# Loading only the weight columns that are used, in a chunked scan of two head groups

## The reference

```
h = rms_norm(x);  proj = h @ w_in
HGRN2 heads (4):   scores[t,s] = sum_d q[t,d] k[s,d] exp(b[t,d] - b[s,d]), s <= t
                   o = scores @ v + (q exp(b)) @ state
DeltaNet heads (4): (I + lower(beta k k^T decay)) solved for u and w, chunk by chunk
                   v_new = u - w @ state;  o = q @ state + attn @ v_new
x += rms_norm(concat(o_a, o_b) @ w_out)
x += rms_norm(gated MLP with a causal convolution (1024 -> 2 x 2816 -> 1024))
x += rms_norm((p @ w_ple) * sigmoid(x @ w_ple_gate))
```

## Time and profile before

| | us |
|---|---|
| three runs | 1464.81, 1464.89, 1466.47 (median 1464.89) |
| the profiled execution, its own time | 1465.47 |
| its span, first to last instruction | 1463.7 |
| scan, from the end of the front to the first matmul of the output projection | about 432 to 596 |
| mean granted TensorE clock, share of full | 0.987 |

### The profile page before, as it was taken

One profiled execution on the slowest core, in us unless ns is written; L12 is line 12 of the kernel. 1 busy time (PEld: TensorE's weight loads), 2 busy tenths in 40 slices (PEclk: granted clock), 3 DMA queues, 4 the chain that ended last, 5 costly groups with the idle time before them and its releaser, 6 DMA issues.

```text
span 1463.7 us, 19613 instructions
## 1 busy us (share of the span) xinstructions
PE 1424.8 (97%) x7167; PEld 1202.3 (82%) x7167; DVE 1029.9 (70%) x1512; ACT 704.1 (48%) x1297; POOL 227.8 (16%) x242
## 2 busy tenths in 40 slices
PE   5999999999999999999999999999999999999996
PEld 4877888878879999888888888888888888888885
DVE  6666545553118888447997999999999685677566
ACT  5432457412226887436774344444445444454434
POOL 3000001100017767110000000000000154310010
PEclk8999999999997999999999999999999999999998
DMA  8553424544712333454442335335326755424222
GB/s 215 86 106 44 43 61 127 152 108 101 165 59 86 100 104 95 143 188 148 148 122 87 103 100 171 116 115 173 107 81 237 249 196 189 137 80 133 84 100 101
DMA packets 156318, 181.52 MB, mean 124 GB/s; under 512 B 21240, under 2 KB 96190, under 8 KB 156222
## 3 DMA queue, kind: packets, MB, share of 16 engines
q1 hardware_dynamic: 155968, 180.16, 42.5%
q10 hardware_dynamic: 254, 0.10, 0.0%
HBM read 130.95 MB, written 49.28 MB: 123 GB/s over the span
## 4 chain that ended last, share of the span: by engine, by line
PE 93%; DVE 3%; ACT 1%; DMA 1%; issue 1%; POOL 0%; SPq 0%; ACTq 0%; DVEq 0%; POOLq 0%
PE psum L2263 10%; PE psum L2264 10%; PE psum L2265 10%; PE psum L563 5%; PE psum L564 5%; PE psum L565 5%; PE psum L1202 5%; PE psum L2202 4%; PE psum L2204 4%; PE psum L2203 4%; PE psum L2175 4%; PE psum L2176 4%; PE psum L2177 4%; PE psum L1256 3%; PE psum L618 3%; PE psum L619 3%
## 5 line engine op out<-in xcount | busy, mean ns | idle before, releaser
L148 DVE TENSOR_TENSOR w_wlo<-w_raw,w_whi 128x1024 fp32r<-128x1024 f32 x70 | 93.8, 1340 | 254.6 <-ACT w_whi L142 254.5
L2263 PE MATMUL psum<-m_hi,w_whi 128*128 128x512 f32 x416 | 162.4, 390 | 1.5 <-issue 0.7
L142 ACT ACTIVATE w_whi<-w_raw 128x1024 fp32r<-128x1024 f32 x70 | 74.0, 1057 | 184.8 <-PE psum L2177 85.4
L2265 PE MATMUL psum<-m_hi,w_wlo 128*128 128x512 f32 x416 | 161.9, 389 | 0.0
L2264 PE MATMUL psum<-m_lo,w_whi 128*128 128x512 f32 x416 | 161.8, 389 | 0.0
L563 PE MATMUL psum<-h_hi,w_whi 128*128 128x512 f32 x320 | 127.0, 397 | 3.7 <-DVE h_lo L834 3.7
L565 PE MATMUL psum<-h_hi,w_wlo 128*128 128x512 f32 x320 | 125.4, 392 | 0.0
L564 PE MATMUL psum<-h_lo,w_whi 128*128 128x512 f32 x320 | 125.4, 392 | 0.0
L2202 PE MATMUL psum<-w_whi,g_slot 128*128 128x512 f32 x308 | 120.1, 390 | 0.6 <-DVE w_wlo L2979 0.6
L2204 PE MATMUL psum<-w_whi,g_slot 128*128 128x512 f32 x308 | 119.8, 389 | 0.0
L2203 PE MATMUL psum<-w_wlo,g_slot 128*128 128x512 f32 x308 | 119.8, 389 | 0.0
(11 more groups left out here) (374 smaller groups left out, 3485.6 us busy)
## 6 DMA issues: line engine op xcount, KB each, us to landing
w_raw<-in_w_up SPq DMA_DIRECT2D x39, 512.0 KB, 3.9
w_raw<-in_w_in SPq DMA_DIRECT2D x36, 512.0 KB, 6.5
s_rows<-pair_work SPq DMA_DIRECT2D x11, 1024.0 KB, 4.1
w_raw<-s_rows SPq DMA_DIRECT2D x44, 256.0 KB, 2.7
g_rows<-pair_work SPq DMA_DIRECT2D x18, 512.0 KB, 2.7
w_raw<-g_rows SPq DMA_DIRECT2D x33, 256.0 KB, 3.2
w_raw<-in_w_out SPq DMA_DIRECT2D x16, 512.0 KB, 4.2
mixed_home<-in_w_down SPq DMA_DIRECT2D x32, 256.0 KB, 3.9
```

What stands on the lines that cost most here:

```text
L2263: pe.matmul(out, wh[:, part], hi(kt), start=(start and kt == 0), stop=False)
L2265: ins = pe.matmul(out, wl[:, part], hi(kt), start=False, stop=(stop and kt == KT // 2 - 1))
```

## The change

Ten products per chunk get weights with fewer columns, and rows of the result with no use are neither computed nor copied. For score level n the weights are the first 128 - 2^(n-1) key columns: 127, 126, 124, 120, 112, 96, 64. Of the inverse, dt32 loads the first 96 columns, dt64 the first 64, y64 the last 64 (its result stands in partitions 64 to 127 of the bank). y32 and dx keep their 128. The copies by DVE and ACT out of these banks are cut to the same partitions. Moving operands, counts of instructions, order, semaphores and transfers stay as they were.

```diff
--- before.py
+++ after.py
@@ -1087,6 +1087,7 @@
     SCORE_BANK = (0, 7, 3, 6, 1, 7, 2, 7)
     BANK_OF = {"ks": 2, "solve": 3, "gd": 3, "og": 4, "oh": 5, "hd": 3, "turn": 2, "mix_g": 2, "mix_h": 5,
                "y32": 6, "dx": 6, "dt32": 1, "y64": 6, "dt64": 7}
+    DT_ROWS, Y64_ROWS = (slice(0, P - SB), slice(0, 2 * SB)), slice(2 * SB, P)
     FIRST_BANK_OF = {"y32": 4, "dx": 5, "dt32": 6, "y64": 4, "dt64": 6}
 
     def __init__(self, nc, k, a, front, shared, heads_on):
@@ -1125,6 +1126,10 @@
     def packed(self, ap):
 
         return ap[:, 0:NH * P // 2].rearrange("p (h t) -> p h t", h=NH)
+
+    def live_keys(self, n):
+
+        return slice(0, P - (1 << (n - 1)))
 
     def packed_blocks(self, ap, m):
 
@@ -1194,12 +1199,12 @@
     def bank(self, name, c):
         return (self.BANK_OF if c else self.FIRST_BANK_OF)[name]
 
-    def pe_products(self, pe, key, bank, left, right, live=None):
-
-        out = self.banks.open(pe, key, bank)
+    def pe_products(self, pe, key, bank, left, right, live=None, rows=slice(0, P)):
+
+        out = self.banks.open(pe, key, bank)[rows, :]
         columns = lambda ap: ap if live is None else self.half(ap, *live)
         for h in range(NH):
-            ins = pe.matmul(columns(self.hs(out, h)), left(h), columns(right(h)), start=True, stop=True)
+            ins = pe.matmul(columns(self.hs(out, h)), left(h)[:, rows], columns(right(h)), start=True, stop=True)
         self.multiplied.mark(ins, key)
 
     def pe_y32(self, pe, c):
@@ -1213,7 +1218,7 @@
         self.banks.released(pe, ("y32", c))
         pe.wait_ge(self.s["xt_in"], (c + 1) * 16)
         self.pe_products(pe, ("dt32", c), self.bank("dt32", c), lambda h: self.hs(self.y, h), lambda h: self.hs(xt, h),
-                         (SB, 1))
+                         (SB, 1), self.DT_ROWS[0])
 
     def pe_dx(self, pe, c):
         xt = self.xt[c % 2]
@@ -1223,13 +1228,13 @@
         self.banks.released(pe, ("dx", c))
         self.banks.released(pe, ("dt32", c))
         self.pe_products(pe, ("y64", c), self.bank("y64", c), lambda h: self.hs(self.lt, h), lambda h: self.hs(self.x, h),
-                         (2 * SB, 0))
+                         (2 * SB, 0), self.Y64_ROWS)
 
     def pe_dt64(self, pe, c):
         xt = self.xt[c % 2]
         self.banks.released(pe, ("y64", c))
         self.pe_products(pe, ("dt64", c), self.bank("dt64", c), lambda h: self.hs(self.y, h), lambda h: self.hs(xt, h),
-                         (2 * SB, 1))
+                         (2 * SB, 1), self.DT_ROWS[1])
 
     def pe_first_inverse(self, pe, step):
 
@@ -1252,8 +1257,9 @@
             pe.wait_ge(s["levels"], c * LEVELS + n)
             at = (c * LEVELS + n - 1) % 3
             out = self.banks.open(pe, ("score", c, n), self.SCORE_BANK[n])
+            live = self.live_keys(n)
             for h in range(NH):
-                ins = pe.matmul(self.packed(out)[:, h, :], hs(self.kl[at], h), self.packed(self.ql[at])[:, h, :],
+                ins = pe.matmul(self.packed(out)[live, h, :], hs(self.kl[at], h)[:, live], self.packed(self.ql[at])[:, h, :],
                                 start=True, stop=True)
             self.multiplied.mark(ins, ("score", c, n))
         else:
@@ -1369,7 +1375,8 @@
             return
         m, key = (SB, 2 * SB)[level], (("y32", "y64")[level], c)
         self.done(act, key)
-        half = lambda ap: self.blocks(heads(ap), m, 0)
+        rows = self.Y64_ROWS if level else slice(0, P)
+        half = lambda ap: self.blocks(heads(ap), m, 0)[rows]
         self.banks.release(act.activation(half(self.y[:]), half(self.banks.of(key)), ACT.Copy), key)
 
     def act_exp(self, act, c, lv):
@@ -1502,8 +1509,10 @@
             self.banks.released(dve, ("dt32", c))
         else:
             self.done(dve, ("dx", c))
-        self.banks.release(dve.copy_predicated(self.blocks(heads(xt[:]), m, 1), self.mask_for(self.k.mask[:, LEVELS - 2 + level, :], m, 1),
-                                               self.blocks(heads(self.banks.of(key)), m, 1)), key)
+        rows = self.DT_ROWS[level]
+        self.banks.release(dve.copy_predicated(self.blocks(heads(xt[:]), m, 1)[rows],
+                                               self.mask_for(self.k.mask[:, LEVELS - 2 + level, :], m, 1)[rows],
+                                               self.blocks(heads(self.banks.of(key)), m, 1)[rows]), key)
 
     def dve_dx(self, dve, c):
         if c >= NT:
@@ -1534,8 +1543,9 @@
         if n:
             self.banks.released(dve, ("score", c, n - 1))
             m = 1 << (n - 1)
-            ins = dve.copy_predicated(self.blocks(heads(self.sc[:]), m, 1), self.mask_for(k.mask[:, n - 1, :], m, 1),
-                                      self.packed_blocks(self.banks.of(key), m))
+            live = self.live_keys(n)
+            ins = dve.copy_predicated(self.blocks(heads(self.sc[:]), m, 1)[live], self.mask_for(k.mask[:, n - 1, :], m, 1)[live],
+                                      self.packed_blocks(self.banks.of(key), m)[live])
         else:
             ins = dve.copy_predicated(heads(self.sc[:]), over_heads(k.ident[:].bitcast(U32)), heads(self.banks.of(key)))
         self.banks.release(ins, key)
```

## The result

The changed kernel takes **1458.49 us** in the median of 4 runs (1456.2 to 1459.18); beside it the kernel before took 1465.68 in 4 (1464.81 to 1467.18). The ratio is 0.995, with a 95% interval of 0.9937 to 0.9962. So it is faster by 7.2 us where 14.3 were forecast, and 1458.49 lies 2 us above the range. The profiled execution took 1458.11 us (span 1456.4), 7.36 less than that of the kernel before.

A forecast was written before the change was run, and what follows sets the result against it. PE bounds the kernel, paced by weight loads at 0.112 us a record. Savings of 0.99 (first inverse), 1.92 (chunk 0), 10.80 (chunks 1 to 6) and 0.60 us (chunk 7) total 14.3: 1450.6 us, range 1447.8 to 1456.5.

The forecast's parts named there:

- What a shorter load is worth: Scan, per chunk: shorter loads of the scores and inverse save 1.80 us, period 19.92 to 18.12 us.
- chunks 1 to 6: Middle of the scan: six chunks at 1.80 us each, 10.80 us saved.
- the price of a column: PE weight loads: each column left out saves 0.83 ns a record, with 0.87 as upper bound.
- Rival 2: Changes between wide and narrow weights cost 0.16 us a pair, 24 pairs, 3.9 us back: 1454.5 us; chance 0.12.
- rival 3: PE empties at each width change, 96 columns included: 40 groups, 0.66 us a pair, 1476.9 us; chance 0.03.
- Rival 1: DVE becomes the bound at 18.9 us a chunk; total gain 9.5 us, 1455.4 us; chance 0.11.
- Rival 4: The 112 ns pace is not the load's, so nothing changes: 1464.9 us; chance 0.05.
- The floor of 63 ns a record: 64-column groups: a record falls from 112 to 63 ns, not 59, saving 0.39 us a group.
- First inverse: Between the projection's slabs, where PE is full: 0.21 + 0.39 + 0.39 = 0.99 us saved.
- Chunk 0: Start of scan: levels 5 to 7, partly at half clock, plus next chunk's dt32 and y64, save 1.92 us.
- the 2 us allowed for it: Start of scan: PE's half-speed clock stretch could end sooner or later, 2 us either way.
- Chunk 7: Earlier savings vanish in PE's wait for DVE before the mixer's turn; levels 6 and 7 behind it save 0.60 us.

The follow-up runs named there:

- four pairs against one: Changed kernel with level 7's four 64-column heads alternating with the mixer's four 128-column transposes in chunks 1 to 7: 1464.54 us, ratio 0.9989.
- the best version: Changed kernel with level 7 and dt64 loading 65 columns, y64 still its last 64: 1453.57 us, ratio 0.9914, period 18.48 us.
- the kernel with 65 columns: Changed kernel with level 7 and dt64 loading 65 columns and y64 all 128: 1454.9 us, ratio 0.9924.

## Why the prediction was wrong

**The step that failed** is in the sum, "What a shorter load is worth": level 7, y64 and dt64 were priced by their eight loads alone, 0.39 us each, with nothing for the two ends of the group. Each end pair costs 0.29 us (0.29 from four pairs against one, 0.285 from 64 against 65 columns, 0.28 from the best version). In chunks 1 to 6, 18 of them are 5.2 of the 5.48 us that are missing (10.80 - 5.32); most of the rest is the price of a column (below). For the whole kernel 24 x 0.29 = 7.0, and 14.3 - 7.0 = 7.3 beside the 7.36 between the two profiled executions, but that this fits so closely is luck: two of the 24 pairs are hidden by chunk 7's wait, and smaller errors make up for them.

**Rival 2 was the mechanism, priced at about half.** It had the 24 pairs and where they lie. Its price, 0.16, was taken from the small transposes, and against a cost at a change of width I held, under rival 3, where 8-column matmuls sit among wide ones without a gap. Those rows are fp32r, the changed groups are plain fp32, and the experiments show that for fp32r even 64 columns are free. I did weigh their 512 moving columns as a reason for doubt; the number type, though I had named it beside the earlier trace rows, I did not weigh, and it was the one that mattered.

**Rival 3**, a drain at every change of width including 96 columns, and slower than before: wrong in both. 96 columns pay nothing (0.70 us a group), and a pair costs 0.29 and not 0.66, under the 0.36 from which it would have decided.

**Rival 1**, DVE: it had room. PE waits for it nowhere in chunks 1 to 6, neither in the changed kernel nor in the version with a period of 18.48. **Rival 4**, a pace that is not the load's: refuted by 0.80 and 0.70 us for 112 and 96 columns.

**Point by point.** The price of a column: load durations give 0.86 ns, near the 0.83 taken, but the pace gained less. Levels 1 to 6 and dt32 brought 0.56 of 0.63 us in their own experiment, and the kernel with 65 columns 1.30 of 1.47: 0.74 ns a column in both. The reason is the first load of each shortened group, which still takes the 0.11 us of the wide one ahead (the first two loads of 65 columns above end after 0.25 us, each of them lasting 0.14), so that seven records of eight gain; 7/8 of 0.83 is 0.73. The floor of 63 ns a record: too high, a group of 65 columns takes 0.53 us, 0.11 to its second record and then 7 x 0.06; by itself that would have made the gain larger.

The Trainium skill ("TensorE: Matmul & The Clock Gate", LDWEIGHTS), whose columns divided by 1.2 GHz the prediction weighed, gives an estimate of 54 ns for 65 columns; the 60 seen agree to 6.

First inverse: 0.99 forecast; PE left its last slab 0.38 us earlier (431.59 to 431.21), which is 0.99 less two pairs to 0.03, and 0.10 of that went into a longer wait for ACT's hgrn_q (0.94 to 1.04 us).

Chunk 0: 1.11 against 1.92, and its terms can't be told apart. Its forecast held 0.39 for y64 of chunk 1. That group lies behind the mark, in the next period, which leaves 1.53; and since chunks 1 to 6 were given a y64 each as well, this one was in truth chunk 7's, which stands ahead of chunk 7's wait and saves nothing. One pair, level 7's, makes it 1.24. The clock then moved: level 7 ran at half speed before (455.66 to 457.36) and at full speed after (455.60 to 456.21; granted 1.00 from 455 to 456, where it was 0.50), while from 447 to 449 the clock was lower after (granted 0.50 for 0.96). In all, half-speed time by the windows was 12.6 + 4.4 us and is 15.5 + 1.6 (granted 0.63 and 0.96), the same 17 us, so the 2 us allowed for it were not needed.

Chunk 7: the longer wait before the turn came as forecast, 0.60 for 0.28, but that its 0.59 us in all agree with 0.60 is luck. From the mark to the end of that wait it took 9.24 us and not 9.41 (572.91 to 582.15, 579.63 to 589.04): 0.17 gained where nothing was forecast. Behind it 0.42 was gained: 0.18 by level 6, 0.09 by level 7 with its ends (what level 7 and the turn behind it save in the middle of the scan), and some 0.14 by a shorter idle stretch ahead of the last HGRN2 outputs.

DVE's waits for PE were to be nearly gone, and they are not: from 473 to 593 us 3.7 us are left of 4.7 ahead of the state's update, and 2.1 of 3.5 ahead of xt's copy. The period shrank by half of what was forecast, so DVE kept more of its room.

The Trainium skill ("TensorEngine Tiling (Array Packing)", Tiling Modes, Key Properties) has a change of tiling mode drain the engine. No trace shows the mode. If a group with 64 or fewer weight columns is such a change, the traces agree for plain fp32, at 0.29 us a pair for 64 columns and with a late start at 32 and 8 too; for fp32r of 64 and 8 columns they do not (0.23 us at every step). Why the price stops between 64 and 65 columns, and why fp32r is spared, stays open. What the traces show is the form of the loss on the way in: the next load is not pulled ahead of the running matmul.

## What to carry to other kernels

Where a PE-bound stretch moves few columns, the weight load sets its pace, and every weight column without a use was worth 0.74 ns for each record here. Cut plain fp32 weights down to 65 columns, not to 64. Where 65 can't be had, as for y64, 64 still paid for eight records together (0.42 us by its loads against 0.28 at the ends), but not for two at a time, so keep narrow ones side by side. And a row that stands as evidence against a cost must share the number type of what is changed, not its shape alone. A step that looks long must be compared with the same step in the kernel before: the 0.33 us behind a group was there all along.

## What the runs showed of the hardware that was not expected

- 65 weight columns are faster than 64: a group of four fp32 products takes 0.53 us against 0.60, and the step into it 0.11 against 0.31.
- The price is a step: 0.42 us for the two records ahead of the group at 64 and at 32 columns, 0.22 at 65.
- fp32r is spared, with 8 and with 64 columns (0.23 us at every step), where the step into plain fp32 of the same shapes takes 0.31 and 0.32, and into plain fp32 of 128 columns 0.23.
- Behind a plain fp32 group the step from the first to the second fp32r matmul of 512 moving columns takes 0.31 to 0.34 us and not 0.23, whatever the width of the group: 128, 65, 64 and 8 columns.
- A group of shorter loads gains on seven records of eight: 0.74 ns a column in the pace where the load durations give 0.86.
